# First block of a two-block network: input weights as fp32r high and low parts, the causal convolution begun beside the projection, attention by pairs of heads on halves of the array

## What is computed

```python
mod = silu(c) @ w_mod + b_mod                      # 6 rows of 1024, w_mod is 1024 x 6144
h = rms_norm(x, g_norm1) * (1 + sc1) + sh1
u = h @ w_in                                       # w_in 1024 x 2560: q, k, v, ga, gb, 512 columns each
q, k, v, ga, gb = split(u)
attn = dilated_attention(q, k, v)                  # 8 heads of 64, causal, ALiBi, three dilations
conv = silu(layer_norm(depthwise_conv31(ga * sigmoid(gb)) + conv_b))
x = x + gt1 * (concat(attn, conv) @ w_out)
```

## Time and profile before

| | |
|---|---|
| median of the runs | 2120.38 us |
| the profiled execution's own time | 2124.13 us |
| its span, first to last instruction | 2122.5 us |
| TensorE, VectorE, ScalarE, GpSimd busy in the span | 1939.1, 1275.2, 1029.4, 179.7 us |
| start and end of the projection's matmuls | 52.1 and 189.5 us |
| start of attention, end of its loop, start of the output stage | 197.5, 295.3, 309.2 us |

### The profile page before, as it was taken

The page is one execution under the profiler, slowest core; times in us unless marked ns, Lnnn a source line. Parts: engine busy times, 40 slices in busy tenths (PEclk is TensorE's granted clock), DMA queues, the critical chain, the costliest instruction groups (busy, mean ns, idle before and its releaser), DMA issues. The chain is left out here.

```text
span 2122.5 us, 28075 instructions
## 1 busy us (share of the span) xinstructions
PE 1939.1 (91%) x10255; PEld 1549.1 (73%) x10255; DVE 1275.2 (60%) x1747; ACT 1029.4 (48%) x1551; POOL 179.7 (8%) x192
## 2 busy tenths in 40 slices
PE   5999889499999999997299999998999989999997
PEld 5444444378888888885287558988999878999886
DVE  4535974688999999995624555744324644544433
ACT  2114761278888888884435654345322333332222
POOL 1101640111111111110110000000000000000000
PEclk9999999599999999998599999999999989999999
DMA  9257700399999999994520101011232212233320
GB/s 358 81 198 263 291 14 30 117 382 376 395 392 388 384 388 389 382 386 164 180 90 21 40 20 61 21 60 56 85 100 98 82 50 80 82 98 100 100 99 40
DMA packets 112085, 368.21 MB, mean 173 GB/s; under 512 B 6991, under 2 KB 61525, under 8 KB 99703
## 3 DMA queue, kind: packets, MB, share of 16 engines
q1 hardware_dynamic: 105094, 344.77, 44.0%
q0 software_dynamic: 6560, 22.02, 3.0%
q10 hardware_dynamic: 338, 0.13, 0.0%
HBM read 333.09 MB, written 33.82 MB: 173 GB/s over the span
## 5 line engine op out<-in xcount | busy, mean ns | idle before, releaser
L1315 DVE TENSOR_TENSOR weight_parts<-fixed,weight_parts 128x1024 fp32r<-128x1024 f32 x384 | 443.0, 1220 | 50.0 <-ACT weight_parts L1268 48.0
L1268 ACT ACTIVATE weight_parts<-fixed 128x1024 fp32r<-128x1024 f32 x384 | 374.9, 1067 | 34.5 <-DMA fixed<-in_w_exp_gate_dram 26.7
L1427 DVE TENSOR_TENSOR weight_parts<-fixed,weight_parts 128x1024 fp32r<-128x1024 f32 x135 | 162.5, 1222 | 211.2 <-ACT weight_parts L1419 211.1
L1528 PE MATMUL psum<-mix_parts,weight_parts 128*128 128x258 f32 (+2 forms) x656 | 206.3, 314 | 9.9 <-DVE weight_parts L1427 6.2
L1528 PE MATMUL psum<-token_parts,weight_parts 128*128 128x264 f32 (+2 forms) x720 | 207.8, 289 | 6.3 <-PEq L1753 3.3
L1199 PE MATMUL psum<-weight_parts,token_parts 128*128 128x512 f32 x512 | 206.1, 403 | 2.4 <-DVE weight_parts L1315 2.2
L1529 PE MATMUL psum<-mix_parts,weight_parts 128*128 128x258 f32 (+2 forms) x656 | 206.9, 315 | 0.0
L1530 PE MATMUL psum<-mix_parts,weight_parts 128*128 128x258 f32 (+2 forms) x656 | 206.0, 314 | 0.0
L1529 PE MATMUL psum<-token_parts,weight_parts 128*128 128x264 f32 (+2 forms) x720 | 205.7, 286 | 0.0
L1530 PE MATMUL psum<-token_parts,weight_parts 128*128 128x264 f32 (+2 forms) x720 | 205.2, 285 | 0.0
L1201 PE MATMUL psum<-weight_parts,token_parts 128*128 128x512 f32 x512 | 200.7, 392 | 0.0
(11 more groups left out here) (419 smaller groups left out, 3545.2 us busy)
## 6 DMA issues: line engine op xcount, KB each, us to landing
fixed<-in_w_exp_gate_dram SPq DMA_DIRECT2D x32, 2048.0 KB
fixed<-in_w_exp_up_dram SPq DMA_DIRECT2D x32, 2048.0 KB, 10.3
fixed<-in_w_exp_down_dram SPq DMA_DIRECT2D x32, 2048.0 KB, 9.7
fixed<-in_w_in_dram SPq DMA_DIRECT2D x26, 1024.0 KB, 5.2
fixed<-in_w_mod_dram SPq DMA_DIRECT2D x12, 2048.0 KB, 12.4
expert_rows<-fixed SPq DMA_DIRECT2D x8, 2560.0 KB, 25.6
fixed<-in_w_ffn_up_dram SPq DMA_DIRECT2D x11, 1024.0 KB, 5.3
fixed<-in_w_ffn_gate_dram SPq DMA_DIRECT2D x11, 1024.0 KB, 5.3
```

The costliest lines, as they stand in the source:

```text
L1268: act.activation(weights[:, 0, piece, :], ring[:, s, q * PIECE:(q + 1) * PIECE], ACT.Copy).then_inc(high_ok, 1)
L1315: dve.tensor_tensor(out, src, high_part.bitcast(F32), ALU.subtract).then_inc(done, 1)
L1427: dve.tensor_tensor(out, raw, high.bitcast(F32), ALU.subtract).then_inc(self.low_ok, 1)
L1528: pe.matmul(out, x(0), w(0), start=start, stop=False)
```

## The change

- `w_in` is loaded in chunks of 1 MB through `Parts` and split into fp32r high and low pieces of 128x1024 (20 pieces, 4 slots); the normed tokens too (`hTP`). Each product is three fp32r matmuls. The order is ga, gb, q, k, then v by rows. ScalarE evaluates each normed tile twice (to a plain copy `htmp` and to the high part).
- `w_mod` has a ring of its own with two slots, `Mods`; its steps on VectorE are dealt out between the pieces. The distance tables are built in the prologue.
- Taps: 4 on TensorE, 20 on GpSimd, 7 on VectorE. In the projection VectorE starts each channel tile (product, seven taps), and the first 44 of GpSimd's 80 additions follow there (`CONV_EARLY`), with products by ScalarE.
- Attention takes two heads at once, 16 steps. Scores are two matmuls on 64 rows of the array each (`kz` is gone). Probabilities aren't divided; a second group of matmuls with ones gives the denominators (`L_BANK`), the two heads' results go to the two halves of the partitions, and VectorE divides once per pair. VectorE copies one of two turned tiles, ScalarE the other.
- The spreading of the sums' rows (eight matmuls) moves into the attention stage's end. `w_out` is loaded at its start, ahead of the stores that zero the experts' rows.

```diff
-PE_TAPS = 12
-POOL_TAPS = 12
+PE_TAPS, POOL_TAPS, DVE_TAPS = 4, 20, 7
...
+MOD_SLOTS = 2
...
+    def load(self, sp, c):
+        if c - MOD_SLOTS in self.read:
+            sem, value = self.read[c - MOD_SLOTS]
+            sp.wait_ge(sem, value)
+        dst, src = columns_chunk(self.w, 512 * c)(self.slots[c % MOD_SLOTS])
+        sp.dma_start(dst, src).then_inc(self.arrived[c % MOD_SLOTS], 16)
...
+CONV_EARLY = 44
+TAP_SLOTS = 4
...
 def input_projection(g):
...
         @block.gpsimd
         def _(pool):
...
+            for k in range(CONV_EARLY):
+                m, _ = tap_of(k)
+                pool.wait_ge(prod_ok, k + 1)
+                pool.tensor_tensor(y[:, m, :], y[:, m, :], taps[k % TAP_SLOTS], ALU.add).then_inc(pool_sum, 1)
+                pool.wait_ge(pool_sum, k + 1)
...
+            for n in range(16):
+                w = parts.use(pe, n)
+                if n >= 4:
+                    pe.wait_ge(taken, n - 3)
+                for k in range(KT):
+                    if n == 0:
+                        pe.wait_ge(h_low, k + 1)
+                    last = three(pe, psum[:, n % 4, :], lambda part: w(part)[:, k, :], lambda part: hTP[:, part, k, :],
+                                 k == 0, k == KT - 1)
+                    if n == 0 and k < 4:
+                        turn_x(g, pe, k + 4).then_inc(xT_ps, 1)
+                last.then_inc(ready, 1)
+                parts.read_by(n, ready, n + 1)
...
+            def products(first, last):
+                for k in range(first, min(last, CONV_EARLY)):
+                    m, tap = tap_of(k)
+                    if k % POOL_TAPS == 0:
+                        act.wait_ge(started, m + 1)
+                    if k >= TAP_SLOTS:
+                        act.wait_ge(pool_sum, k - TAP_SLOTS + 1)
...
+            for n in range(16):
+                take(n)
+                parts.high(act, n + W_SLOTS)
+                if n >= 6:
+                    goal = CONV_EARLY * (n - 5) // 13
+                    products(done, goal)
+                    done = goal
+            products(done, CONV_EARLY)
+            for n in range(16, 20):
+                take(n)
...
+            for n in range(16):
+                parts.low(dve, n + W_SLOTS)
+                if 5 <= n <= 8:
+                    conv(n - 5)
+                else:
+                    mod_steps(4 if n < 5 else 6)
+            mod_steps(8 * KT)
...
 def attention_and_conv(g):
...
+            def scores(s):
+                pair, i = divmod(s, TT)
+                if s:
+                    pe.wait_ge(s_sb, 2 * s)
+                n = (i + 1) * P
+                for r in range(2):
+                    row = slice(HD * r, HD * r + HD)
+                    pe.matmul(psum[:, S_BANK + r, 0:n], qT[row, pair, i * P:n], kT[row, pair, 0:n],
+                              start=True, stop=True).then_inc(s_ps, 1)
...
+                for bank in (L_BANK, O_BANK):
+                    for j in range(TT):
+                        for r in range(2):
+                            h = 2 * pair + r
+                            w = v[:, j, h * HD:(h + 1) * HD] if bank == O_BANK else ones[:, 0:HD]
+                            last = pe.matmul(psum[HD * r:HD * r + HD, bank, j * P:], w, PT[pair % 2][:, r, j, j * P:],
+                                             start=(j == 0), stop=(j == TT - 1))
...
+            scores(0)
+            for s in range(STEPS + 1):
+                if s + 1 < STEPS:
+                    scores(s + 1)
+                if s < STEPS:
+                    conv_tap(s)
+                if s:
+                    turn(s - 1)
+                    if s > 1 and (s - 1) % TT == 0:
+                        values((s - 1) // TT - 1)
+            pe.wait_ge(s_sb, 2 * STEPS)
+            mod_rows(0)
+            mod_rows(1)
+            values(PAIRS - 1)
+            pe.wait_ge(y_done, CM)
...
+            def out(pair):
+                dve.wait_ge(o_ps, pair + 1)
+                step(dve.reciprocal(rl, psum[:, L_BANK, :]))
+                dve.tensor_tensor(mixA[:, pair, :], psum[:, O_BANK, :], rl, ALU.mult).then_inc(o_sb, 1)
+
+            tables(0)
+            for s in range(STEPS + 1):
+                if s < STEPS:
+                    scores(s)
+                if s % TT == 0 and s:
+                    finish_tile(s // TT - 1)
+                if s:
+                    dst, src = take_probs(dve, s - 1, 1)
+                    dve.tensor_copy(dst, src).then_inc(pt_sb[1], 1)
+                if s % TT == 2 and s // TT + 1 < PAIRS:
+                    tables(s // TT + 1)
+                if s % TT == 2 and s // TT:
+                    out(s // TT - 1)
+            out(PAIRS - 1)
```

859 lines of the change are left out of this document (432 added, 427 removed).

## The result

After: 2135.81 us (median of 4, 2131.83 to 2136.45). Before, timed with it: 2121.11 us (median of 4, 2119.68 to 2125.11). Ratio 1.0057, interval 1.0039 to 1.0076 (the two medians alone would give 1.0069): slower, as forecast, but by 12 to 15 us, about half of the 26 us forecast. The profiled execution of after took 2136.45 us with a span of 2134.7, that of before 2124.13 with 2122.5, so the two traces differ by 12.2 us.

| | before | forecast | after |
|---|---|---|---|
| attention starts | 197.5 | 205 | 199.5 |
| last turn of the loop ends | 295.3 | 316 | 295.8 |
| output stage starts | 309.2 | 336 | 317.0 |
| from there to the end of the span | 1813.3 | 1813.3 | 1817.7 |

What follows compares the result with a forecast made beforehand. TensorE alone bounded the projection, and four engines were near full in the loop. Projection end 205, loop 111 and tail 20 gave 336 us against 309.2, rounded to +26; less 3.8 for the base, 2146 us, range 2103 to 2176.

Steps and rivals of the forecast that it cites:

- changes of shape: Attention loop, TensorE: 0.15 us for each change of matmul tile shape, 34 changes, 5 us.
- step (7): Output stage and all code behind it: unchanged length, 1813.3 us.
- turns between VectorE and GpSimd: Projection: two-input VectorE instructions and GpSimd additions take turns, 1.13 us for GpSimd and 0.55 for VectorE.
- a ring in the loop: Attention loop: scores, additions, tap, turn and copy wait on each other, so a step is their sum; sixteen steps 66.5 us.
- Prologue: Before the projection: two modulation slots instead of four make the scale ready at 47.5 us instead of 46.3, +1 us.
- term (d): Projection: each of 44 early GpSimd additions costs a VectorE without gaps 0.89 us, 39 us in all.
- rival A: Projection: the turns don't bite, TensorE's 109 us count and it ends at 168; 2109 us, faster, chance 0.22.
- clock: Attention loop: TensorE at half clock for two steps after each of four idle gaps, less overlap with values, 8 us.
- values, three pairs: Attention loop, TensorE: each pair's values and sums 4.5 us less 1.5 hidden, 9 us for three pairs.
- tails and signals: Attention loop: record ends and handovers between engines, 4 x 0.43 = 1.7 us over four steps, an estimate.
- Rival C: Attention loop: the ring is looser, a step near 3.0 us with TensorE ahead; -24 us, 2122, about the same, chance 0.11.
- Tail: Between loop and output stage: from 13.9 to about 20 us, with row sums, values, mean and squares' sum.

Runs made afterwards that it cites:

- e1: After with its 44 early GpSimd additions left out and only their signals kept: attention starts at 166.4 us instead of 199.5, whole 2099.95 us (one run).
- e13: After with seven unread row sums added on TensorE behind the turn of steps 6, 10 and 14: loop and tail 115.6 us against 117.5, whole 2127.30 (one run).
- e14: After with two unread row sums (1.7 us) added at the tail's end: 2133.15 us, code behind 1811.5 instead of 1817.7.
- e15: Before with two unread row sums (1.7 us) added ahead of the unchanged code: 2125.41 us, code behind 1817.6 instead of 1813.3.
- e5: After with the 36 GpSimd additions of the attention loop left out, signals and products kept: loop and tail 117.8 us against 117.5, whole 2135.81 (one run).
- e8: After with TensorE's order changed to tap, turn, next scores, then values: loop and tail 107.5 us against 117.5, whole 2123.52.
- e10: e8 with VectorE finishing conv tiles before its additions, tables made while waiting for the turn, reciprocals halved over two steps: loop and tail 97.2 us, whole 2110.80.

## Why the prediction was right in sign and wrong in size

Three steps of it failed. The steps of the attention loop with their changes of shape were put at 71.5 us and took about 57; the price of an early addition in the projection was put at 0.89 us and was 0.75; and step (7), the unchanged code behind, was put at no change and came out 4.4 us longer. The mechanisms, turns between VectorE and GpSimd and a ring in the loop, were right.

**Prologue: right.** The scale was ready at 47.3 us, 47.5 forecast.

**Projection: mechanism right, price too high.** TensorE alone 168, measured 166.4 with no additions (e1). The term (d), 44 x 0.89 = 39 us, measured 33.1. Where the two alternate without a gap the price is 1.56 less 0.78, 0.78 us, not 0.89, which for 44 would be 34. The stage ended 5.5 us before the 205 forecast. With 33 us above 26, rival A's point (15 of 44 additions) was passed.

**Loop: ring right, its steps 14 us too long.** Forecast 111, measured 96.3. In after the steps of a pair, each from the start of its scores (128, 256, 384 and 512 columns) to the start of the next, take 5.13, 4.43, 6.58 and 10.75 us (from 240.10), 26.9 together. The values are 4.46 of the third, tables, reciprocal and product 2.39 + 3.36 + 0.69 = 6.4 of the fourth, and the half clock is 1.9 of the first (e13). That leaves 14.1 us for four steps at full clock, where 16.6 and 1.25 for the changes of shape had been forecast. The terms of the loop:

| | forecast | measured |
|---|---|---|
| 16 steps, changes of shape with them | 66.5 + 5 | 57, what is left of 96.3 |
| clock | 8 | 6 (e13) |
| values, three pairs | 9 | 3 x 4.46 = 13.4 |
| tables | 8.7 | 3 x 2.39 = 7.2 |
| reciprocal and product | 12.3 | 12.2 |
| start | 1.5 | in the steps |
| sum | 111 | 96.3 |

Of the 14 us on the steps, three parts can be read. The scores came at the lower bound (both heads' records begin together and a pair of 512 columns takes 1.06 us in all), 1.1 us less for four steps. The additions took 3.5 instead of 4.1 us (14.0 for 32). And in the third step VectorE's copy and additions, 1.3 us, lie beside the values while I had added them. With these three the four steps would be 13.6 us; 14.1 were measured, so of the 1.25 for changes of shape about 0.5 is seen (256.24 to 257.30 is 1.06 us for 0.86 of columns), the rest I read as counted already in the 0.43 us for tails and signals; no run separates the two. I had put such an overlap on the values instead, 1.5 us of each: on TensorE nothing of them is hidden, 4.4 us more than forecast. The clock's 8 us were about right. Rival C, a looser ring, isn't what happened: TensorE waits for the additions and VectorE for the turn in every step but the one with the values.

**Tail: 20 forecast, 21.2 measured,** one more: it began at half clock, which alone is 1.6 (two row sums 3.48 us, 1.88 in e13). I had said that the last reciprocal hides beside the row sums; it ended at 307.67 with its product, and the mean was ready at 307.0.

**Behind: step (7) failed.** 4.4 us that the forecast had at nothing. e14 and e15 show that as much comes and goes with no change of that code, by where TensorE runs at half clock; what decides where isn't shown.

**The base.** I took 3.8 us off because the profiled execution of before lay above its median; that of after lies 0.6 above its own, so 3.1 came back. The errors together: -5.5 - 14.7 + 1.2 = -19.0 for the start of the output stage (336 to 317.0), 0.8 of it given back by my rounding of 26.8 to 26, +4.4 behind and +3.1 by the base: -10.7, from 2146 to 2135.3; 2135.8 was measured.

## What to carry to other kernels

An addition that GpSimd makes beside a busy VectorE costs VectorE about the time of one of its own instructions, 0.75 us for 512 columns here, so nothing is saved by moving it there; in a stage where VectorE waits for others most of an addition's cost is hidden (36 of them cost about 3 us, e5). When each step of a loop becomes a chain through two engines, look at the order in each queue before the sizes: the turn ahead of the scores gave 10 us (e8), and VectorE's tables, tile and reciprocal put where it waited 10 more (e10), with the same work. In such a ring a wait is not slack: TensorE waited 30.7 us for the additions, and half clock still cost about 6 us. And before two traces are compared, look whether they had parted already where their code is the same, as e13 and after had by 3 us.

## What the runs showed of the hardware

The same code behind the changed part, 1813.3 us in before, took from 1810.3 to 1817.7 us in the seventeen traces, with 153 to 174 us of it at half clock. A difference of 4 us between two kernels of 2100 is therefore no evidence on a part; the start of the next stage is, since attention started at 199.0 to 200.8 in the ten traces with the same code ahead of it.

Two float32 tiles on the two halves of the array's rows or columns ran in the time of one (2.37 us for 16 records and for 8). A GpSimd copy reading one tile cost VectorE 0.17 us, an addition reading two 0.75. At half clock a step of the loop took 5.12 us instead of 3.24, another 5.56 instead of 4.43.
